# TensorE asks once whether an expert has overflowed, and the closing products stand directly behind that question

## The reference, cut to what matters

```python
gu = jnp.einsum("td,edf->tef", h, w_expert_gu)
act = jax.nn.silu(gu[..., :EXPERT_DIM]) * gu[..., EXPERT_DIM:] * combine[..., None]
routed = jnp.einsum("tef,efd->td", act, w_expert_down)
...
f = moe(...)                       # routed + shared
x = x + gate_f * rmsnorm(f, g_post_ffn)
```

## Time and profile before

| | |
|---|---|
| median of 3 runs | 799.47 us (797.45 to 802.65) |
| the profiled execution, own time | 796.85 us |
| its span, first to last instruction | 794.7 us |
| TensorE busy | 741.6 us, 93% of the span |
| VectorE busy | 419.6 us, 53% |
| ScalarE busy | 225.8 us, 28% |
| mean granted TensorE clock | 0.975 of full speed |
| last product of group 27 to first closing product | 772.58 to 776.41 us |
| last instruction of VectorE's tail ends | 791.64 us |

### The profile page before, as it was taken

The page is one execution under the profiler, slowest core; times in us unless marked ns, Lnnn a source line. Parts: engine busy times, 40 slices in busy tenths (PEclk is TensorE's granted clock), DMA queues, the critical chain, the costliest instruction groups (busy, mean ns, idle before and its releaser), DMA issues.

```text
span 794.7 us, 12271 instructions
## 1 busy us (share of the span) xinstructions
PE 741.6 (93%) x4613; PEld 452.7 (57%) x4613; DVE 419.6 (53%) x1003; ACT 225.8 (28%) x383; POOL 84.9 (11%) x48
## 2 busy tenths in 40 slices
PE   1689979999999899999999999999999999999984
PEld 1589867787856455555544445555444545555442
DVE  3178988576185655445444544445445445445444
ACT  3135213474261122222222222222222222222232
POOL 2235344412310000000000000000000000000000
PEclk9879979999999999999999999999999999999997
DMA  9996475534495469999999999999999999899711
GB/s 325 375 360 228 135 289 212 194 126 153 140 354 234 154 252 362 350 410 428 401 428 422 376 386 423 398 423 431 387 428 421 389 425 408 358 427 426 314 55 81
DMA packets 47263, 256.05 MB, mean 322 GB/s; under 512 B 6240, under 2 KB 8896, under 8 KB 30432
## 3 DMA queue, kind: packets, MB, share of 16 engines
q1 hardware_dynamic: 39360, 247.47, 77.9%
q0 software_dynamic: 1664, 4.35, 1.7%
q10 hardware_dynamic: 6176, 3.40, 1.5%
HBM read 253.07 MB, written 2.13 MB: 321 GB/s over the span
## 4 chain that ended last, share of the span: by engine, by line
PE 77%; DVE 9%; DMA 7%; ACT 3%; issue 1%; SPq 1%; POOL 1%; DVEq 0%; ACTq 0%
PE psum L1911 25%; PE psum L1940 12%; PE psum L1866 10%; PE psum L1883 9%; PE psum L1875 3%; DMA w_gu<-in_w_expert_gu 3%; DMA w_gu<-in_w_ada 3%; PE psum L495 3%; PE psum L1793 3%; PE psum L497 3%; PE psum L496 3%; DVE psum L1021 2%; DMA w_gu<-in_w_in 2%; PE psum L1810 1%; SPq L563 1%
## 5 line engine op out<-in xcount | busy, mean ns | idle before, releaser
L1911 PE MATMUL psum<-w_gu,hgT 128*32 128x512 f32 (+1 forms) x1344 | 198.1, 594 | 2.0 <-DMA w_gu<-in_w_expert_gu 1.3
L1410 DVE TENSOR_TENSOR f_acc<-f_acc,psum 128x512 f32<-128x512 f32 x168 | 115.4, 687 | 49.9 <-PE psum L1883 49.8
L1911 PEld LDWEIGHTS psum<-w_gu,hgT 128*32 128x32 f32 (+1 forms) x1344 | 60.7, 119 | 136.4 <-issue 135.4
L1940 PE MATMUL psum<-w_dn,actT 128*32 128x512 f32 (+1 forms) x672 | 102.1, 596 | 0.0
L1401 DVE TENSOR_TENSOR y_lo<-psum,y_hi 128x1024 fp32r<-128x1024 f32 x28 | 34.3, 1225 | 106.7 <-ACT y_hi L888 106.7
L490 POOL TENSOR_TENSOR w_lo<-w_gu,w_hi 128x2048 fp32r<-128x2048 f32 x14 | 64.2, 4590 | 71.9 <-ACT w_hi L647 71.9
L1866 PE MATMUL psum<-h_hi,onehot 128*128 128x512 f32 x174 | 71.1, 409 | 0.0
L1883 PE MATMUL psum<-y_hi,onehotT 128*128 128x512 f32 x168 | 70.4, 419 | 0.0
L1866 PE MATMUL psum<-h_lo,onehot 128*128 128x512 f32 x174 | 68.0, 391 | 0.0
L1393 DVE SCALAR_TENSOR_TENSOR act<-sil,wsl,psum 128x256 f32<-128x256 f32 x28 | 19.1, 680 | 89.5 <-ACT sil L883 89.4
L1883 PE MATMUL psum<-y_lo,onehotT 128*128 128x512 f32 x168 | 66.1, 394 | 0.0
(11 more groups left out here) (292 smaller groups left out, 956.8 us busy)
## 6 DMA issues: line engine op xcount, KB each, us to landing
w_gu<-in_w_expert_gu SPq DMA_DIRECT2D x64, 2048.0 KB, 13.2
w_dn<-in_w_expert_down SPq DMA_DIRECT2D x64, 1024.0 KB, 10.2
w_gu<-in_w_ada SPq DMA_DIRECT2D x12, 2048.0 KB, 16.9
w_gu<-in_w_in SPq DMA_DIRECT2D x4, 2048.0 KB, 12.3
w_gu<-in_w_out SPq DMA_DIRECT2D x2, 2048.0 KB, 8.5
bc<-mod_rows POOLq DMA_DIRECT2D x6, 512.0 KB, 7.1
w_gu<-in_w_in SPq DMA_DIRECT2D x2, 1024.0 KB, 16.1
w_gu<-in_w_shared_gu SPq DMA_DIRECT2D x1, 2048.0 KB, 9.2
```

The costliest lines, as they stand in the source:

```text
L1410: v.tensor_tensor(dst, dst, bank(5 + n), ALU.add).then_inc(f_added, 1)
L1911: ins = t.matmul(bank(2)[rows, :], hgT[:, c, rows], w_gu[s][:, c, :], start=(c == 0), stop=(c == NC - 1), tile_position=(0, rows.start))
L1940: ins = t.matmul(bank(3 + n)[rows, :], actT[:, j, rows], w_dn[s][:, j, 512 * n:512 * (n + 1)], start=(j == 0), stop=(j == 1), tile_positio ...
```

## The change

Only TensorE's list changes. It reads `n_pairs` and branches on `n_pairs < 1`. In the first arm stand the closing's waits, with constants for numbers, and the closing itself, once, for the buffer that group 27 uses (`(GROUPS - 1) % 2`, which is 1). In the other arm stand the load of `odd`, the overflow groups and the closing as it was. The branch on `n_pairs > 0` ahead of the first overflow group is gone, since the arm implies it. At the end of the first arm stands an unconditional branch over the whole other arm.

```diff
-            t.wait_ge(tab_ready, 1)
-            n_pairs = t.value_load(table_e[0:1, N_TAB:N_TAB + 1], min_val=0, max_val=OVER_PAIRS)
-            odd = t.value_load(table_e[0:1, N_TAB + 1:N_TAB + 2], min_val=0, max_val=1)
-            with t.If(n_pairs > 0):
-                over(0, 0)
-            with t.Else():
-                t.nop()
-            with t.If(n_pairs > 1):
...
-            t.wait_ge(f_added, n_pairs * 6 + (6 * GROUPS + 6))
-            t.wait_ge(hgT_ready, n_pairs * 2 + (2 * GROUPS + 2))
-            total_so_far(0)
-            total_so_far(1)
-            t.wait_ge(wsl_ready, n_pairs + (GROUPS + 1))
-            total_so_far(2)
-            t.wait_ge(ohT_ready, n_pairs + (GROUPS + 1))
-            t.wait_ge(y_ready, n_pairs + (GROUPS + 1))
-            with t.If(odd > 0):
-                all_outputs(0)
+            t.wait_ge(tab_ready, 1)
+            n_pairs = t.value_load(table_e[0:1, N_TAB:N_TAB + 1], min_val=0, max_val=OVER_PAIRS)
+            with t.If(n_pairs < 1):
+                t.wait_ge(f_added, 6 * GROUPS + 6)
+                t.wait_ge(hgT_ready, 2 * GROUPS + 2)
+                total_so_far(0)
+                total_so_far(1)
+                t.wait_ge(wsl_ready, GROUPS + 1)
+                total_so_far(2)
+                t.wait_ge(ohT_ready, GROUPS + 1)
+                t.wait_ge(y_ready, GROUPS + 1)
+                all_outputs((GROUPS - 1) % 2)
             with t.Else():
-                all_outputs(1)
+                odd = t.value_load(table_e[0:1, N_TAB + 1:N_TAB + 2], min_val=0, max_val=1)
+                over(0, 0)
+                with t.If(n_pairs > 1):
...
```

More of the change, by code:

```diff
@@ L2003, in all_outputs @@
                 last_outputs(par, 2)
-            t.wait_ge(f_added, n_pairs * 6 + (6 * GROUPS + 6))
-            t.wait_ge(hgT_ready, n_pairs * 2 + (2 * GROUPS + 2))
-            total_so_far(0)
-            total_so_far(1)
-            t.wait_ge(wsl_ready, n_pairs + (GROUPS + 1))
-            total_so_far(2)
-            t.wait_ge(ohT_ready, n_pairs + (GROUPS + 1))
-            t.wait_ge(y_ready, n_pairs + (GROUPS + 1))
-            with t.If(odd > 0):
-                all_outputs(0)
-            with t.Else():
-                all_outputs(1)
+            t.wait_ge(tab_ready, 1)
[10 more added lines that the diff above has]
+                all_outputs((GROUPS - 1) % 2)
+            with t.Else():
+                odd = t.value_load(table_e[0:1, N_TAB + 1:N_TAB + 2], min_val=0, max_val=1)
+                over(0, 0)
+                with t.If(n_pairs > 1):
+                    over(0, 1)
+                    with t.Fori(1, OVER_PAIRS // 2) as jj:
+                        for q in range(2):
+                            with t.If(jj * 2 + q < n_pairs):
+                                over(jj, q)
+                            with t.Else():
+                                t.nop()
+                with t.Else():
+                    t.nop()
+                t.wait_ge(f_added, n_pairs * 6 + (6 * GROUPS + 6))
+                t.wait_ge(hgT_ready, n_pairs * 2 + (2 * GROUPS + 2))
+                total_so_far(0)
+                total_so_far(1)
+                t.wait_ge(wsl_ready, n_pairs + (GROUPS + 1))
+                total_so_far(2)
+                t.wait_ge(ohT_ready, n_pairs + (GROUPS + 1))
+                t.wait_ge(y_ready, n_pairs + (GROUPS + 1))
+                with t.If(odd > 0):
+                    all_outputs(0)
+                with t.Else():
+                    all_outputs(1)
 _INS = ["x_prompt", "x_sample", "state_C", "state_n", "state_m", "c", "c_ctx", "w_ada", "b_ada", "g_pre_mix", "w_in",
```

## The result

The changed kernel takes 795.31 us in the median of 14 runs (792.67 to 799.8), the kernel before 799.85 in 14 runs beside it. The ratio is 0.9944, 95% interval 0.9923 to 0.9964: 4.5 us faster, where 4.9 were forecast, and inside 1%. Ratios in this document leave out executions more than 1.5% above the fastest of the same kernel: none in this pair, one of 4294 us with the added products and one of 802.13 us with tile 0 first, both further down.

What follows compares the result with a forecast made beforehand. The prediction took the chain of waits after TensorE's last group as the bound, with 3.83 us of "issue" from L1974. Terms 3.83 + 1.17 - 0.1 = 4.9 us took the median 799.47 to 794.6 us, range 792 to 798.

Steps and rivals of the forecast that it cites:

- steps 1 to 3: TensorE ahead of the closing: L1974 removed, one untaken branch kept, first closing product directly after L1940; gain 3.83 us.
- both bounds I had set: Cost of TensorE's kept, untaken branch: between 0.37 us (taken, short code) and 5.25 us (the far one).
- one far fetch, priced by the distance: L1974 on TensorE jumps over three overflow groups to code not at hand, which is fetched: 5.25 us against L1970's 0.37.
- The rival of the 5.25 us at any branch: L1974's 5.25 us are a sequencer wait any branch there would have, no fetch; gain nothing, 799.5 us; chance 0.04.
- step 4: TensorE's six `total_so_far` passes run at full clock, without idling before: 2.58 us instead of 3.75, gain 1.17 us.
- step 5: The first `last_outputs` on TensorE waits for `y_ready`, just covered by 0.2 us; 0.1 us charged for the handover.
- The limit of 5.2 us: Any gain beyond 5.2 us would be cut off by TensorE's wait for `y_ready`.
- step 6: VectorE is ready by 778, before its tail's first gate product, L1478, would start at 778.45.
- two small packets: Instruction-queue packets near 775.5 and 777.9, read as code for VectorE and the next piece, fetched once it ran again.
- step 7: The added unconditional branch at the end of TensorE's arm stalls 5.25 us but costs nothing, with 7.7 us of cover.

Runs made afterwards that it cites:

- the added products: The kernel before, with four filler products nobody reads put ahead of TensorE's load of `n_pairs`; ratio to before 1.001.
- tile 0 first: The changed kernel with tile 0's products, `y_hi` and `y_lo` included, finished before `total_so_far(2)`; ratio to before 0.9924.
- the run without it: The kernel before, with TensorE's overflow groups left out of its list and both branches kept; ratio to before 0.9942.
- the run with `y_hi` first: The changed kernel with tile 0's two `y_hi` products waiting for `y_hi` alone, ahead of the wait for `y_ready`; ratio to before 0.9943.
- arms exchanged: The changed kernel with TensorE's branch asking `n_pairs > 0`, overflow groups directly behind it and the closing in the other arm; ratio to before 0.9962.
- one group behind the second branch: The kernel before, with the loop of two overflow groups left out behind TensorE's second branch, L1974; one execution, 801.1 us.

## Why the prediction was right, and where its terms were off

- *The gap is L1974's, and the fall-through removes it* (steps 1 to 3): right. 3.90 us by the products' starts, forecast 3.83. The untaken branch took 86 ns, below both bounds I had set from taken ones. What I didn't see is that the fall-through itself is worth only 1.00 us: a single long jump, asked for 1.08 us earlier, leaves 0.94 us of the gap and keeps the clock up.
- *What L1974 waits for.* That code between is the price is shown by the run without it (0.2 us per branch). That it was one far fetch, priced by the distance, was too simple: one farther jump took 3.54 us, and a jump no longer than L1970's took 3.41. The other 1.7 us go with a second packet, not with closeness alone, since two jumps as close to each other took 0.37 and 3.41 with one packet. That L1970's look-ahead is the packet in the way stays a reading. The Trainium skill's rule ("Runtime: NRT & Kernel Launch", Instruction fetch mechanics) names the jump out of the window; the trace agrees in kind, with a packet beside each jump of 3.3 us and more, and shows prices from 3.3 to 5.25 us.
- *The rival of the 5.25 us at any branch, beside which the 108 ns of the Trainium skill stood*: fell with the same run. That figure of the Trainium skill ("Advanced Engine Details and Errata", Control Flow Timing) lies between what the traces show on TensorE for a branch not taken, 86 ns, and for a taken one without a stall, 207 to 370 ns.
- *The clock* (step 4): right in kind, mis-sized. I took 1.17 us; the filler run measured 1.51 for the same six passes. I had set six passes of 0.43 against the 3.75 us up to the first `y_hi` weight load, but that load comes while the last pass still runs: at full clock it stood 2.25 us behind the first pass (780.27 - 778.02), not 2.58.
- *What is late next* (step 5): right that `y_ready` is just covered, by 0.2 us in the forecast and 0.15 measured (+6.01 against +6.16). The 0.1 us that I charged for the handover isn't there, as the run with `y_hi` first shows. What holds tile 0 is TensorE's own third `total_so_far`, and once that is behind it, `y_ready` and VectorE. The limit of 5.2 us was too low by what the clock was under-priced; the stretch gained 5.43.
- *VectorE ready in time* (step 6): right, by 0.27 us. The reading of its two small packets held, as far as the runs show: the first moved with VectorE's question, and VectorE was ready at about +8.7, ahead of the second (+8.97 before), while TensorE's 5.25 us behind its branch would have made it +11.2.
- *The jump at the arm's end* (step 7): it is there, 3.66 us and not 5.25, and costs nothing on TensorE. On VectorE, whose tail stands at the end of the program, such a jump stood ahead of its drain for 3.1 us.
- *The sum*: 4.9 forecast, 5.43 in the stretch, 4.5 (2.9 to 6.2) in whole times. The missing half microsecond of the stretch is the clock's 0.34, the 0.1 of step 5 and 0.07 of the handover. That 4.9 and 4.5 lie so close is partly luck: the interval of whole times would have taken 3 or 6 as well, and only the stretch tests the terms.

## What to carry to other kernels

Look at the sequencer's own lines where a chain says "issue": a branch of several us there was, in every case here, one with an instruction packet beside it. Ask once, as early as the work already handed over can cover; that gave 4.43 of the 5.43 us. Let the usual case fall through for the rest, but put the jump that this moves to the arm's end on an engine that isn't last. Before moving more, ask when the next engine in line is ready behind its own jump.

## What the runs showed of the hardware

A branch on TensorE's sequencer cost 0.09 us untaken, 0.21 to 0.37 us taken without a stall, 3.3 to 3.9 us with one 16 KB packet on the instruction queue, and 4.70 and 5.25 us where two packets went over. On VectorE the way out of two jumps took 2.7 us. After 3.8 us of idling TensorE ran most of its next six float32 passes at half clock and lost 1.5 us; after 0.94 us (arms exchanged) and 1.99 us (one group behind the second branch) it lost none.
